# The state space part of a two-block kernel: 130 chunks of 8 tokens for 65 chunks of 16, a scan in two levels, and tables built between the first products

## The chip, the cores and the metric

One core of a Trainium2 chip runs the kernel. The metric is device time in microseconds of one execution; lower is better. The engines work side by side, each on its own queue in order, and meet at semaphores: TensorE (PE; its weight loads are PEld), VectorE (DVE), ScalarE (ACT), GpSimd (POOL) and SyncE (SP), which here only issues the weight loads.

## What is computed

Two transformer blocks on 1024 tokens of width 1024. The first puts 16 meta tokens ahead (so 1040 tokens), projects, runs causal differential attention on half of the width and a state space model on the other half, and mixes both. The part that the change touches is the state space model: 32 groups of 16 channels, 64 complex states each.

```python
def s5_ssm(u, a_re, a_im, log_dt, b_re, b_im, c_re, c_im, d_skip):
    dt = jnp.exp(log_dt)[:, None]
    mag, ang = jnp.exp(a_re * dt), a_im * dt
    ab_re, ab_im = mag * jnp.cos(ang), mag * jnp.sin(ang)
    ...                                   # bb = f * b, f from ab and a
    bu_re = jnp.einsum('blgh,gph->blgp', u, bb_re)
    bu_im = jnp.einsum('blgh,gph->blgp', u, bb_im)
    ...                                   # x_t = ab * x_(t-1) + bu_t, complex, by associative_scan
    y = (jnp.einsum('blgp,ghp->blgh', x_re, c_re) - jnp.einsum('blgp,ghp->blgh', x_im, c_im))
    y = y + d_skip.reshape(N_SSM_GROUPS, SSM_GROUP) * u
    return y.reshape(bsz, length, N_SSM_GROUPS * SSM_GROUP)
```

The queries and keys get a partial rotation (`rope`): out = t cos + rot(t) sin on the first quarter of each head. Behind both halves come a gated unit on y (glu), the mixing product, a feed-forward, and the second block (retention and RWKV-7, feed-forward, gate). None of these is changed.

## The kernel before

**Staging.** Activations lie in SBUF with features on partitions, split in a high and a low fp32r part (`act_hi`, `act_lo`); each large product is three passes over (high, high), (low, high), (high, low). Weights come as units of 128 x 1024 in the order `ORDER` through six slots (`SLOTS`); SP loads a unit when the one six places ahead of it is done, POOL splits it (`split_to`, L522 and L524). Every engine runs the same order of events, written out by hand: generators are advanced by the lists `PROJ_EVENTS` and `HEAD_EVENTS`, so an engine does its share of one event, then of the next. `give` starts an instruction and waits for its own end, `take` waits for another engine's.

**First stretch.** After the first norm, `PROJ` lists 29 products: u for 4 units with 3 spans each (512, 512 and 16 columns), v for 4 token tiles and the meta rows, then q and k for 8 units (one span for the first four, a second one of 16 columns for the others). Products rotate over three PSUM banks; ACT takes each out. A q or k unit is then rotated: PE multiplies `qk_raw` by `rot`, DVE makes `qk_o` out of it (`rotated`, three operations), ACT stores `qk_o` (L728). When the u units are stored, eight DMAs bring them back as `u_in` [128, 32 groups, 130], with 8 tokens x 16 channels on the partitions (L705).

**State space part, tables.** The groups are worked two to a pair of partition halves (16 pairs), four groups to a batch (`TB` = 8 batches). A chunk is `STEP` = 16 tokens, so there are 65 chunks, each of two octets. DVE discretises (`discretise`) and makes the powers `pw` of the state factor up to 16 (L2297 on). For each batch b:

- DVE `build_factors(b)`: `ca`, power times C for 17 lags, seven operations on 544 columns (L2084, L2087), after the store of the last one has landed;
- PE: impulse response kd = bb x ca, 16 instructions of 256 columns (L1478), then 8 transposes of the input factors `g_t` (L1489) that POOL makes (`input_factors`, L536);
- DVE copies kd out of PSUM, adds d_t (L2327 on), and copies the turned factors to `gt` (L2331); ACT stores `ca` and `kd` (L775, L778);
- PE: chunk inputs S = gt x u_in, 32 instructions of 65 columns (L1501); DVE copies them to `xs` (L2337).

In `PROJ_EVENTS` these stand after 15 products, as ssm, proj, ssm, proj for each batch.

**State space part, scan and output.** While attention's first half runs (`attention(0)`, 69 steps, with the far half of the v, q and k products between them, L1424 and L1676), DVE scans: for each chunk after the first, four operations on 32 columns (`wx`, `xs`), 63 times, in 8 parts, a part in every other attention step. Then, in every sixth step, PE makes a batch of output (L1520, L1522, L1524): for a group two blocks (even and odd octets), from `m_t` (shifted copies of kd, loaded by 8 DMAs a batch) and `ca2` (the stored `ca`) with `xs`; ACT copies `yb` out and stores it. An fp32 product is two instructions in the trace.

## Time and profile before

| | us |
|---|---|
| median of three runs | 3815.72 (3814.40 to 3825.63) |
| the profiled execution | 3815.3 |
| its span, first to last instruction | 3813.3 |
| PE busy | 3271.4 (86%) |
| PEld busy | 2539.4 (67%) |
| DVE busy | 1795.7 (47%) |
| ACT busy | 924.8 (24%) |
| POOL busy | 1995.2 (52%) |

Times in views of the trace count from the start of the span. A stretch's row gives busy time and in brackets the number of instructions for PE, PEld, DVE, ACT and POOL, then the granted clock (1.00 is 2.4 GHz, 0.50 is 1.2 GHz; between them a mix), the DMA share and GB/s. A row of a timeline gives start, length, engine, line, operation, output tile <- input tiles, shapes and count, and in brackets how long the engine had been idle and what ended it. Line 2084 is the helper for all of DVE's two-input operations, so the tile tells which it is; L626 is the same for ACT.

### The profile page before, as it was taken

What the parts mean: (1) busy time and instruction counts of PE and PEld (TensorE: products, weight loads), DVE (VectorE), ACT (ScalarE), POOL (GpSimd) and SP (SyncE); (2) the same over time, 40 slices, a digit from 0 to 9 for tenths busy, and PEclk for the clock granted to TensorE, in tenths of its full rate; (3) what the DMA queues carried; (4) which work ended last, traced back from release to release, by engine and by line L of the source; (5) the groups of instructions that cost most, each with busy time, mean ns of one, the idle gap of its engine ahead of it and who ended that gap; (6) DMA issues with size and microseconds to landing.
All of it is one profiled execution on the core that took longest, in us unless ns stands there. A gap on an engine that the chain in (4) does not pass through costs nothing.

```text
span 3813.3 us, 48913 instructions
## 1 busy us (share of the span) xinstructions
PE 3271.4 (86%) x19888; PEld 2539.4 (67%) x19888; DVE 1795.7 (47%) x2574; ACT 924.8 (24%) x1625; POOL 1995.2 (52%) x1076
## 2 busy tenths in 40 slices
PE   5874789569999785998889998898899998899997
PEld 4653466447777564776767776676677777678885
DVE  5366422233343354176556655257656556322233
ACT  3000111223233223213223332412223322210012
POOL 4452211225555463674655665565566665567773
PEclk9976677679999897999999999899999999999998
DMA  3521222222221232432222224232222222322221
GB/s 123 112 76 58 59 66 75 84 74 67 83 77 66 69 122 95 156 103 72 69 66 66 77 70 149 100 128 82 71 76 84 76 70 71 125 79 94 94 100 61
DMA packets 143856, 328.19 MB, mean 86 GB/s; under 512 B 25376, under 2 KB 62432, under 8 KB 143632
## 3 DMA queue, kind: packets, MB, share of 16 engines
q1 hardware_dynamic: 58752, 213.94, 16.8%
q10 hardware_dynamic: 84880, 111.12, 9.4%
q8 instruction: 158, 2.59, 0.3%
q14 instruction: 66, 0.54, 0.0%
HBM read 281.88 MB, written 43.12 MB: 85 GB/s over the span
## 4 chain that ended last, share of the span: by engine, by line
PE 72%; DVE 18%; ACT 4%; DMA 2%; ACTq 2%; issue 2%; POOL 0%; DVEq 0%; POOLq 0%
PE ps L1676 28%; PE ps L1705 11%; PE ps L1717 11%; PE ps L1907 3%; PE ps L1443 2%; PE ps L1540 2%; PE ps L1524 1%; DVE act_lo L2084 1%; DVE cab L2084 1%; DVE acc_dense L2084 1%; DVE wx L2084 1%; DVE ffh_lo L2713 1%; PE ps L1568 1%; PE ps L1520 1%; DVE rq L2084 1%
## 5 line engine op out<-in xcount | busy, mean ns | idle before, releaser
L522 POOL TENSOR_TENSOR w_hi<-w_raw,ones 128x1024 fp32r<-128x1024 f32 x408 | 807.7, 1980 | 1491.3 <-DMA w_raw<-weights 1477.3
L524 POOL TENSOR_TENSOR w_lo<-w_raw,w_hi 128x1024 fp32r<-128x1024 f32 x408 | 1005.1, 2464 | 32.0
L1676 PE MATMUL ps<-act_hi,w_hi 128*128 128x512 f32 x1696 | 709.3, 418 | 7.2 <-DVE act_lo L2084 6.6
L1676 PE MATMUL ps<-act_lo,w_hi 128*128 128x512 f32 x1696 | 683.7, 403 | 0.0
L1676 PE MATMUL ps<-act_hi,w_lo 128*128 128x512 f32 x1696 | 678.7, 400 | 0.0
L1676 PEld LDWEIGHTS ps<-act_hi,w_hi 128*128 128x128 f32 x1696 | 327.4, 193 | 101.0 <-issue 16.4
L1676 PEld LDWEIGHTS ps<-act_hi,w_lo 128*128 128x128 f32 x1696 | 327.0, 193 | 76.2
L1676 PEld LDWEIGHTS ps<-act_lo,w_hi 128*128 128x128 f32 x1696 | 326.8, 193 | 67.6 <-issue 1.7
L2084 DVE TENSOR_TENSOR acc_dense<-acc_dense,ps 128x512 f32<-128x512 f32 x352 | 242.1, 688 | 234.4 <-PE ps L1705 175.1
L1705 PE MATMUL ps<-w_hi,ffh_hi 128*128 128x512 f32 x704 | 295.4, 420 | 59.4 <-DVE acc_dense L2084 56.2
L626 ACT ACT_TABLE_LOAD x204 | 261.7, 1283 | 294.5 <-PE ps L1676 108.1
L1705 PE MATMUL ps<-w_hi,ffh_lo 128*128 128x512 f32 x704 | 281.8, 400 | 0.0
L1705 PE MATMUL ps<-w_lo,ffh_hi 128*128 128x512 f32 x704 | 281.3, 400 | 0.0
L1717 PE MATMUL ps<-w_hi,act_hi 128*128 128x512 f32 x640 | 264.0, 412 | 10.1 <-issue 5.6
L1717 PE MATMUL ps<-w_hi,act_lo 128*128 128x512 f32 x640 | 258.4, 404 | 0.0
L1717 PE MATMUL ps<-w_lo,act_hi 128*128 128x512 f32 x640 | 256.4, 401 | 0.0
L2709 DVE TENSOR_TENSOR ff_f<-ff_f,ps 128x512 f32<-128x512 f32 x88 | 60.5, 687 | 310.8 <-PE ps L1676 309.5
L1705 PEld LDWEIGHTS ps<-w_hi,ffh_hi 128*128 128x128 f32 x704 | 136.4, 194 | 101.3 <-DVE acc_dense L2084 67.3
L2173 DVE TENSOR_REDUCE small<-ps 128x1 f32<-128x144 f32 (+7 forms) x64 | 49.6, 775 | 303.3 <-PE ps L1542 303.2
L1705 PEld LDWEIGHTS ps<-w_lo,ffh_hi 128*128 128x128 f32 x704 | 136.3, 194 | 31.1
L1717 PEld LDWEIGHTS ps<-w_hi,act_hi 128*128 128x128 f32 x640 | 124.9, 195 | 43.8 <-issue 10.3
L1705 PEld LDWEIGHTS ps<-w_hi,ffh_lo 128*128 128x128 f32 x704 | 136.7, 194 | 25.7
(369 smaller groups left out, 4934.5 us busy)
## 6 DMA issues: line engine op xcount, KB each, us to landing
w_raw<-weights SPq DMA_DIRECT2D x408, 512.0 KB, 3.3
rw<-rw_t ACTq DMA_DIRECT2D x24, 256.0 KB, 2.2
rw<-lora_t ACTq DMA_DIRECT2D x24, 256.0 KB, 2.0
ca_scratch<-ca ACTq DMA_DIRECT2D x8, 544.0 KB, 2.9
ca<-ca_scratch ACTq DMA_DIRECT2D x8, 544.0 KB, 4.0
row<-x ACTq DMA_DIRECT2D x8, 512.0 KB, 3.3
m_t<-kd_scratch ACTq DMA_DIRECT2D x64, 64.0 KB, 3.5
row_dense<-x ACTq DMA_DIRECT2D x8, 512.0 KB, 3.9
```

Source lines behind the costliest of these rows:

```text
L522: pool.tensor_tensor(w_hi[:, s], raw, ones[:, 0:1].to_broadcast([P, 1024]), MUL).then_inc(w_hi_made, 1)
L524: pool.tensor_tensor(w_lo[:, s], raw, w_hi[:, s].bitcast(F32), SUB).then_inc(w_ready, 1)
L626: return act.activation(out, in_, func, **kw)
L1443: mm = pe.matmul(ps[:, n % 3, 0:c1 - c0], ws[w][:, u % SLOTS, P * k:P * k + P], acts[a][:, k, c0:c1], start=(k, w, a) == (0, 0, 0), stop=( ...
L1540: mm = pe.matmul(out[:, c:c + w], q, k[:, META + c:META + c + w], start=True, stop=True)
L1676: mm = pe.matmul(out, ws[w][:, s, P * k:P * k + P], acts[a][:, k, x], start=(k, w, a) == (0, 0, 0), stop=(k, w, a) == (KT - 1, 1, 0))
L1705: mm = pe.matmul(ps[:, 2 + n % 2, :], ffh[a][:, m % 4, P * k:P * k + P], ws[w][:, s, BANK * j:BANK * j + BANK], start=(m % 2, w, a) == (0, ...
L1717: mm = pe.matmul(ps[:, kinds[2] + k, :], source[a][:, 2 * uu + kk, x], ws[w][:, pos % SLOTS, BANK * kk:BANK * kk + BANK], start=(uu, kk, w ...
L1907: mm = pe.matmul(ps[head(c), 4 + b, n * u:n * u + n], lhs[head(c), u], rhs[head(c), u], start=True, stop=True)
L2084: give(dve.tensor_tensor(out, a, b, op), signal)
L2173: give(dve.tensor_reduce(small[:, col:col + 1], score_rows(h, u, br), X_AXIS, ALU.max, negate=True), s_max)
L2709: give(dve.tensor_tensor(ff_f[:, m % 2], ff_f[:, m % 2], ps[:, 1, :], MUL), ff_prod)
```

## The change

A chunk is now an octet of 8 tokens: 130 chunks, nine powers (`LAGS` 9), and one square impulse block of 128 x 128 to a group instead of a block of two octets. What follows from it, part by part:

- **Tables.** `ca`, `g_t` and `kd` are double. `ca` has 288 columns an operation, six operations with C negated beforehand (`c_n`). DVE builds batches 0 and 1 at once and batch b + 2 in event b. d_t is added on PE, by a small product with the identity; ACT copies kd, gt and xs out of PSUM. POOL splits 6 weight units (8 before) ahead of the first input factors, and up to unit 8 + b behind batch b (10 + b before).
- **Order.** The kd blocks go between the fourth and the twelfth product; three v products follow; then for each batch turn, state product, two projection products.
- **Scan.** 10 blocks of 13 chunks. First the powers of the chunk factor (`run_powers`), then 12 steps inside all blocks at once, nine steps over the block ends, then the ends spread into the blocks: 11 parts, one in each of the first 11 attention steps. ACT loads the first output tables only after the scan.
- **Output.** One block to a group: a product with `m_t` and two with `ca2`, 130 columns each, again one batch in every sixth step.
- **Rotation in place.** `qk_o` is gone; DVE rotates in `qk_raw`, and ACT, before it takes out a product of q or k, waits for the store of the unit two before.
- The loads of `u_in` go one v product earlier, with `rope`'s load behind them.

```diff
-STEP = 16
-NSTEP = L // STEP
 OCT = 8
 NOCT = L // OCT
+BLOCKS, RUN = 10, NOCT // 10
 PAIRS = GROUPS // 2
 GB = 8
-LAGS = STEP + 1
+LAGS = OCT + 1
...
-    PROJ_EVENTS = ["proj", "ssm"] + ["proj"] * 14 + ["ssm", "proj", "ssm", "proj"] * TB
+    PROJ_EVENTS = ["proj", "ssm"] + ["proj"] * 3 + ["ssm", "proj"] * TB + ["proj"] * 3 + ["ssm", "ssm", "proj", "proj"] * TB
     assert PROJ_EVENTS.count("proj") == len(PROJ) + 2
...
-        extra = ([["ssm"]] + [[]]) * (SCAN_PARTS + 1) + ([[]] * 5 + [["ssm"]]) * TB
+        extra = [["ssm"]] * (SCAN_PARTS + 1) + ([[]] * 5 + [["ssm"]]) * TB
...
-        split_to(8)
+        split_to(6)
         pool.wait_ge(factors_ready, 1)
         for b in range(TB):
             input_factors(b)
-            split_to(10 + b)
+            split_to(8 + b)
...
-                    if m == 2:
+                    if m == 1:
                         spills_landed(1)
                         for e in range(OCT):
                             act.dma_start(u_in[SG * e:SG * e + SG], t["u_scratch"][:, :, e, :].rearrange("m (g h) c -> h (m g) c", h=SG)).then_inc(ssm_landed, 16)
+                        act.dma_start(rope[:, :, :], t["rope"][:, :, 0:NEAR]).then_inc(const_landed, 16)
...
-                        act.wait_ge(rope_done, rope_index(m - 1, 0))
+                        store_turned(m - 2)
+                        act.wait_ge(qk_stored[m % 2], 16 * (m // 2))
                     act.wait_ge(*proj_done(n))
                     give(fn(qk_raw[:, m % 2, c0:c1], src, ACT.Copy, scale=QK ** -0.5 if m < 4 else 1.0), proj_kept)
...
+                if b:
+                    act.wait_ge(ca_stored, 16 * b)
+                    act.wait_ge(kd_stored, 16 * b)
+                act.dma_start(t["ca_scratch"][b], ca[:, b % 2]).then_inc(ca_stored, 16)
+                take(kd_psum)
+                for j in range(2):
+                    out = fn(kd[:, b % 2, j:TG:2, P:], ps[0:SG, 4 + 2 * (b % 2) + j, 0:2 * P].rearrange("p (g n) -> p g n", g=2), ACT.Copy)
+                    give(out, kd_ready if j else act_step)
+                act.dma_start(t["kd_scratch"][:, TG * b:TG * b + TG, :], kd[:, b % 2]).then_inc(kd_stored, 16)
+                yield
+            for b in range(TB):
+                q = slice(TQ * b, TQ * b + TQ)
+                take(g_turned)
+                give(fn(gt[:, :, :, :].rearrange("p q r n -> p (q r n)"), ps[:, 6, :], ACT.Copy), gt_ready)
...
+                take(ssm_s)
+                for ri in range(2):
+                    give(fn(xs[:, ri, q, 1:NOCT + 1], ps[:, 7 - ri, 0:TQ * NOCT].rearrange("p (q c) -> p q c", q=TQ), ACT.Copy), ssm_x if ri else act_step)
...
+            act.wait_ge(ssm_scanned, 1)
...
-                    rows, q = slice(SN * (g % 2), SN * (g % 2) + SN), g // 2
+                    rows, q, bank, c0 = slice(SN * (g % 2), SN * (g % 2) + SN), g // 2, 4 + 2 * (b % 2) + j % 2, P * (j // 2)
+                    skip = slice(SN * (g % 2), SN * (g % 2) + SG)
                     for ri in range(2):
-                        mm = pe.matmul(ps[0:SG, 4 + j % 2, 256 * (j // 2):256 * (j // 2) + 256], bb[rows, ri, q],
-                                       ca[rows, ri, q % TQ, 0:STEP, :].rearrange("p l h -> p (l h)"), start=ri == 0, stop=ri == 1)
+                        pe.matmul(ps[0:SG, bank, c0:c0 + P], bb[rows, ri, q], ca[rows, b % 2, ri, q % TQ, 0:OCT, :].rearrange("p l h -> p (l h)"),
+                                  start=ri == 0, stop=ri == 1)
+                    mm = pe.matmul(ps[0:SG, bank, c0:c0 + SG], ident[skip, skip], d_t[skip, q],
+                                   start=False, stop=True, skip_group_check=True)
                 post(mm, kd_psum)
+                yield
+            for b in range(TB):
                 pe.wait_ge(g_ready, b + 1)
+                pe.wait_ge(*((ssm_x, b) if b else (kd_ready, TB)))
                 for n in range(TQ):
-                    if b and n == 0:
-                        pe.wait_ge(gt_ready, TQ * (b - 1) + 1)
-                    if b and n == 1:
-                        pe.wait_ge(ssm_x, b)
-                    for half in range(2):
-                        for ri in range(2):
-                            mm = pe.transpose(ps[:, 6 + n, P * (2 * half + ri):P * (2 * half + ri) + P],
-                                              g_t[:, ri, n, OCT * half:OCT * half + OCT, :].rearrange("p s h -> p (s h)"), ident[:, :])
-                    post(mm, g_turned)
+                    for ri in range(2):
+                        mm = pe.transpose(ps[:, 6, P * (2 * n + ri):P * (2 * n + ri) + P], g_t[:, b % 2, ri, n].rearrange("p s h -> p (s h)"), ident[:, :])
+                post(mm, g_turned)
                 yield
                 if b == 0:
-                    pe.wait_ge(ssm_landed, 16 * (5 + OCT))
-                pe.wait_ge(gt_ready, TQ * (b + 1))
+                    pe.wait_ge(ssm_landed, 16 * (6 + OCT))
+                pe.wait_ge(gt_ready, b + 1)
                 for ri in range(2):
                     for n in range(TQ):
                         for par in range(2):
-                            rows, c0 = slice(SN * par, SN * par + SN), NSTEP * (TQ * ri + n)
-                            for half in range(2):
-                                mm = pe.matmul(ps[rows, 7, c0:c0 + NSTEP], gt[:, n, half, ri, rows],
-                                               u_in[:, TG * b + 2 * n + par, half:NOCT:2], start=half == 0, stop=half == 1)
+                            rows = slice(SN * par, SN * par + SN)
+                            mm = pe.matmul(ps[rows, 7 - ri, NOCT * n:NOCT * n + NOCT], gt[:, n, ri, rows], u_in[:, TG * b + 2 * n + par, :], start=True, stop=True)
                 post(mm, ssm_s)
...
+                    out = ps[:, 2 + j % 2, NOCT * (j // 2):NOCT * (j // 2) + NOCT]
+                    pe.matmul(out, m_t[:, j, :], u_in[:, g, :], start=True, stop=False)
+                    for ri in range(2):
+                        mm = pe.matmul(out, ca2[rows, ri, q % TQ, 1:LAGS, :].rearrange("p l h -> p (l h)"), xs[rows, ri, q, 0:NOCT], start=False, stop=ri == 1)
...
-            tt(qk_o[:, m % 2, c0:c1], qk_raw[:, m % 2, c0:c1], rope[:, 0, c0:c1], MUL)
-            tt(qk_o[:, m % 2, c0:c1], qk_o[:, m % 2, c0:c1], rope_sin_part[:, 0:c1 - c0], ADD, rope_done)
+            tt(qk_raw[:, m % 2, c0:c1], qk_raw[:, m % 2, c0:c1], rope[:, 0, c0:c1], MUL)
+            tt(qk_raw[:, m % 2, c0:c1], qk_raw[:, m % 2, c0:c1], rope_sin_part[:, 0:c1 - c0], ADD, rope_done)
...
+            if b >= 2:
+                dve.wait_ge(kd_psum, b - 1)
+                dve.wait_ge(ca_stored, 16 * (b - 1))
             lags = lambda ri: pw[:, ri, q, :].unsqueeze(3).to_broadcast([P, TQ, LAGS, SG])
-            chan = lambda ri: c_t[:, ri, q, :].unsqueeze(2).to_broadcast([P, TQ, LAGS, SG])
-            tmp = cab[:, :, :].rearrange("p a (q l h) -> p a q l h", q=TQ, l=LAGS)
-            cmul(ca[:, 0], ca[:, 1], lags(0), lags(1), chan(0), chan(1), tmp[:, 0], tmp[:, 1], negate_im=True, last=ca_ready)
+            chan = lambda c, ri: c[:, ri, q, :].unsqueeze(2).to_broadcast([P, TQ, LAGS, SG])
+            one, two = [cab[:, n].rearrange("p (q l h) -> p q l h", q=TQ, l=LAGS) for n in range(2)]
+            tt(one, lags(0), chan(c_t, 0), MUL)
+            tt(two, lags(1), chan(c_t, 1), MUL)
+            tt(ca[:, b % 2, 0], one, two, SUB)
+            tt(one, lags(0), chan(c_n, 1), MUL)
+            tt(two, lags(1), chan(c_n, 0), MUL)
+            tt(ca[:, b % 2, 1], one, two, ADD, ca_ready)
...
+        def run_powers():
+            give(dve.tensor_copy(px[:, 0, :, 0], a_step[:, 0, 0]), dve_step)
+            give(dve.tensor_copy(px[:, 1, :, 0], a_step[:, 1, 1]), dve_step)
+            wide = lambda v, n: v.unsqueeze(2).to_broadcast([P, PAIRS, n])
+            scratch = local[:, :].rearrange("p a r q i -> p a (r q i)")
+            for have, n in ((1, 1), (2, 2), (4, 4), (8, RUN - 8)):
+                tmp = scratch[:, :, 0:PAIRS * n].rearrange("p a (q h) -> p a q h", h=n)
+                cmul(px[:, 0, :, have:have + n], px[:, 1, :, have:have + n], wide(px[:, 0, :, have - 1], n), wide(px[:, 1, :, have - 1], n),
+                     px[:, 0, :, 0:n], px[:, 1, :, 0:n], tmp[:, 0], tmp[:, 1])
+            both_ways(a_run, px[:, :, :, RUN - 1], dve_step)
+
+        def scan_within(steps):
+            x = xs[:, :, :, 1:NOCT + 1].rearrange("p r q (i j) -> p r q i j", j=RUN)
+            now, other = local[:, 0], local[:, 1]
+            factor = lambda n: a_step[:, n].unsqueeze(3).to_broadcast([P, 2, PAIRS, BLOCKS])
+            for j in steps:
+                tt(now, x[:, :, :, :, j - 1], factor(0), MUL)
+                tt(other, x[:, ::-1, :, :, j - 1], factor(1), MUL)
+                tt(now, now, other, ADD)
+                tt(x[:, :, :, :, j], x[:, :, :, :, j], now, ADD)
+
+        def scan_ends(blocks):
+            now, other = wx[:, 0:2, :], wx[:, 2:4, :]
+            for i in blocks:
+                before, end = RUN * i, RUN * i + RUN
+                tt(now, xs[:, :, :, before], a_run[:, 0], MUL)
+                tt(other, xs[:, ::-1, :, before], a_run[:, 1], MUL)
+                tt(now, now, other, ADD)
+                tt(xs[:, :, :, end], xs[:, :, :, end], now, ADD)
+
+        def scan_spread(part, signal):
+            q = slice(4 * part, 4 * part + 4)
+            x = xs[:, :, q, 1:NOCT + 1].rearrange("p r q (i j) -> p r q i j", j=RUN)
+            shape = [P, 4, BLOCKS - 1, RUN - 1]
+            end = lambda ri: x[:, ri, :, 0:BLOCKS - 1, RUN - 1].unsqueeze(3).to_broadcast(shape)
+            power = lambda ri: px[:, ri, q, 0:RUN - 1].unsqueeze(2).to_broadcast(shape)
+            one, two = spread_tmp[:, 0], spread_tmp[:, 1]
+            for ri in range(2):
+                out = x[:, ri, :, 1:BLOCKS, 0:RUN - 1]
+                tt(one, end(ri), power(0), MUL)
+                tt(two, end(1 - ri), power(1), MUL)
+                tt(one, one, two, ADD if ri else SUB)
+                tt(out, out, one, ADD, signal if ri else dve_step)
...
+                if b + 2 < TB:
+                    build_factors(b + 2)
+                yield
+            for b in range(TB):
+                yield
+                yield
+            run_powers()
+            yield
+            dve.wait_ge(ssm_x, TB)
+            for part in range(4):
+                scan_within(range(1 + 3 * part, 4 + 3 * part))
+                yield
+            for blocks in (range(1, 6), range(6, BLOCKS)):
+                scan_ends(blocks)
```

## Rows read from the trace of the kernel before

**Rows 1.** By stretch: length; PE, PEld, DVE, ACT, POOL busy (instructions); clock; DMA share; GB/s.

```profile
57.00:132.00 75.00, 74.90 (x360) 62.37 (x360) 22.88 (x73) 12.68 (x17) 23.97 (x14) 0.98 0.27 75
132.00:311.00 179.00, 123.10 (x809) 85.58 (x808) 118.32 (x141) 7.29 (x15) 107.14 (x66) 0.80 0.36 89
...
324.00:414.00 90.00, 43.61 (x125) 29.55 (x126) 66.92 (x287) 9.15 (x33) 4.24 (x2) 0.59 0.06 22
414.00:442.60 28.60, 24.49 (x86) 15.31 (x86) 11.62 (x20) 5.90 (x20) 12.73 (x6) 0.80 0.38 103
442.60:688.20 245.60, 217.81 (x860) 162.50 (x858) 61.61 (x127) 35.58 (x113) 34.26 (x16) 0.70 0.22 64
```

**Rows 2.** TensorE's timeline: start us, length, line, operation, count, [idle before it <- releaser].

```profile
132.10 1.91 PE L1478 MATMUL ps<-ca,bb 64*16 64x256 f32 x16
...
151.46 2.06 PE L1501 MATMUL ps<-u_in,gt 128*64 128x65 f32 x32 [10.85 <-DMA u_in<-u_scratch]
...
300.11 3.60 PE L1478 MATMUL ps<-ca,bb 64*16 64x256 f32 x16 [17.05 <-DVE ca L2087]
...
323.97 0.79 PE L1540 MATMUL ps<-k_pair,q_pair 64*128 64x128 f32 x2 [6.78 <-DMA k_pair<-qk_scratch]
```

**Rows 3.** The chain of work from 0 to 700 us: start, length, what.

```profile
57.10 58.29 PE ps L1443 x288
...
182.95 5.59 PE ps L1443 x24
```

**Rows 4.** ScalarE's timeline, its DMA issues (ACTq) among it.

```profile
78.10 1.13 ACT L626 ACTIVATE u_t<-ps 128x512 f32<-128x512 f32 x1 [5.39 <-PE ps L1443]
...
129.36 9.24 ACTq L705 DMA_DIRECT2D u_in<-u_scratch  x8
...
152.06 0.60 ACT L626 ACTIVATE v_o<-ps 128x512 f32<-128x512 f32 x1 [12.81 <-DMA v_scratch<-v_o]
...
311.14 0.33 ACTq L728 DMA_DIRECT2D qk_scratch<-qk_o  x1
```

**Rows 5.** VectorE's timeline, around the end of the discretisation.

```profile
78.74 2.71 DVE L2084 TENSOR_TENSOR cab<-pw 128x64 f32<-128x64 f32 x2
...
81.75 0.62 DVE L2084 TENSOR_TENSOR cab<-pw 128x128 f32<-128x128 f32 x2
...
85.38 1.48 DVE L2084 TENSOR_TENSOR cab<-pw,c_t 128x544 f32<-128x544 f32 x2
```

**Rows 6.** GpSimd's groups, 56 to 312 us: count | busy us, mean ns | idle before.

```profile
L524 POOL TENSOR_TENSOR w_lo<-w_raw,w_hi 128x1024 fp32r<-128x1024 f32 x16 | 41.0, 2559 | 1.3
...
L536 POOL TENSOR_TENSOR g_tmp<-pw,bb 128x512 f32<-128x512 f32 x32 | 35.0, 1092 | 57.8 <-PE ps L1489 55.9
L522 POOL TENSOR_TENSOR w_hi<-w_raw,ones 128x1024 fp32r<-128x1024 f32 x16 | 34.5, 2159 | 75.6 <-DMA w_raw<-weights 75.1
```

**Rows 7.** The page's DMA issues: KB each, median us to landing.

```profile
ca_scratch<-ca ACTq DMA_DIRECT2D x8, 544.0 KB, 2.9
```

**Rows 8.** Groups from 324 to 443 us: a scan operation.

```profile
L2084 DVE TENSOR_TENSOR wx<-xs,a 128x32 f32<-128x32 f32 x126 | 26.7, 212 | 4.3
```

**Rows 9.** Busy time in stretches that are one output block each.

```profile
442.60:457.50 14.90, 14.90 (x59) 12.97 (x57) 0.00 (x0) 1.00 (x2) 4.25 (x2) 0.50 0.10 35
...
606.70:616.80 10.10, 10.10 (x59) 8.80 (x57) 4.33 (x5) 0.40 (x1) 3.77 (x2) 0.81 0.01 2
```

**Rows 10.** TensorE's timeline, fp32 products of 128 columns.

```profile
325.37 0.77 PE L1540 MATMUL ps<-k_pair,q_pair 64*128 64x128 f32 x2
...
331.91 0.47 PE L1540 MATMUL ps<-k_pair,q_pair 64*128 64x128 f32 x2
...
688.10 2.07 PE L1568 MATMUL ps<-v_pair,a_t 128*128 128x128 f32 x8
...
798.45 1.27 PE L1568 MATMUL ps<-v_pair,a_t 128*128 128x128 f32 x10
```

**Rows 11.** Waits from 414 to 693 us: in total, times, longest.

```profile
PE ps L1595 <- DVE o_n L2091: 24.6, 10, 10.1
```

157 lines of the change are left out of this document (59 added, 98 removed).

## The prediction

> **What bounds the kernel now.** I read the busy time by stretches first [rows 1]. The change touches the work up to about 688 us only; what stands behind it (glu, the feed-forwards, the second block: 3125 us) keeps its instructions, and I give it no change. Four stretches matter. From 57 to 132 TensorE is the bound (74.9 of 75.0 us busy with the u and v products). From 132 to 311 nobody is: PE is busy 123 of 179 us, DVE 118. There the state space tables are built group batch by group batch in a ring: DVE builds `ca`, PE multiplies, DVE copies out, ACT stores, DVE may build again. The last turn of this ring shows it: PE sat idle 17.05 us until DVE had written `ca` [rows 2]. From 324 to 414 DVE is the bound (66.9 us busy, and most of the rest it waits for the PE work of the attention steps): the 63 steps of the scan stand between the attention steps. From 442.6 to 688.2 PE is the bound (217.8 of 245.6 us), at a granted clock of 0.70, and the eight output blocks of the state space part (L1520, L1522, L1524) are the largest single thing in it.
>
> **Start, +1.** ACT's queue gets one more constant load (d_t in two halves of small pieces) ahead of the wait that lets the first norm begin. Bound: 0 to +3 us; I take +1, since a load costs about 0.5 us to issue there.
>
> **Projection, -21.** The tables' product blocks (kd) move from between the qk products to between the u products, the turns and state products stay, and copies go to ACT. I follow the new order on PE.
> The u products take 58.3 us for four units, so 14.6 for a unit, 5.6 for a product of 512 columns [rows 3]. Four products are done at 77.8 (ACT gets the fourth at 78.10) [rows 4]. Then the first kd block needs `ca`. Before, DVE began it at 85.38. The last power stage goes (L2084 128x128, from 81.75: 2.0 us); POOL no longer splits a weight unit meanwhile (it stops at 6 units and waits for the factors), which gives back 3.9 us (two operations on 64 columns took 2.71, two on 128 took 0.62) [rows 5]; `c_n` adds 0.3. So it begins at 79.8. Its six operations have 288 columns instead of 544 (0.74 each, half of 1.48): 0.46 each by the line through 128 and 544 columns. POOL starts the input factors at the same moment; I double them: 5.5 us. PE can go on at 85.3, having waited 7.5.
> A kd block: sixteen instructions of 128 columns for sixteen of 256, and eight small ones for d_t. The old block took 1.91 us at full clock and 3.60 at the low one [rows 2]. Bounds 1.4 to 4.0; I take 2.2, nearer the fast one, since PE comes from dense products: eight make 17.6. DVE builds two batches ahead into the double tables and has 5 to 8 us for each 3 to 5 us build, so PE shouldn't wait for it again. With 37.6 us of u products left, PE reaches the v products at 140.5 and has three of them at 157.
> Then it waits for the inputs `u_in`. Before, the loads were issued from 129.36 and had landed at 151.46, 22.1 us later [rows 2, 4]. Now they are issued behind the first v store, at about 149: landed at 171, and with ACT's copy of the turned factors the first state product starts at 172.5. This wait is as long as before (some 15 us); it hides nothing new.
> From there: state product 1.5 (the first of before took 2.06 with twice the instructions of half the columns), v3 5.6, the meta rows 6.5 (as many instructions, begun after a pause), to 186. Rounds 1 and 2 (turn 0.5, ACT copy 0.8, state product 1.5, two products 11.2, a rotation 0.9): 14.9 each, to 216. In rounds 3 to 5 a weight unit is late: POOL begins it only behind the input factors, and these behind the turn of the same round. Factors: six operations, the products 1.09 us at 512 columns, about 0.6 now, 3.8 in all; the split of a unit 2.16 + 2.56 [rows 6]: 8.5 us from the turn, of which PE covers 2.3. So 6 us of stall, 18.2 a round, to 271. Round 6 12.3, round 7 with two rotations 4, DVE 3: the last rotated piece is ready at 290, where before its store was issued at 311.14, 12.8 us ahead of the first scores at 323.97 [rows 2, 4]. So the scores start at 303 instead of 324: -21. Bounds: -35 (kd at 1.4, no unit late, `u_in` faster) to -3 (kd at 4, DVE doubled again by POOL, the stall 10).
> The moved copies: per batch 0.35 us twice for kd, 0.6 for gt, 0.35 twice for xs, on an engine that is busy 7.3 of 179 us [rows 1]; at nothing, except the 0.8 us in each round above, where PE waits for the copy. Behind ACT's new waits for stores to land stand its evacuations of products; the margin is a product's 5.6 us against a landing of 2.9 for the `ca` store [rows 7].
> By the Trainium skill, page "SBUF — State Buffer", section "SBUF: two separate sides", DVE with two SBUF inputs and GpSimd hold their common ports as an exclusive lock for a whole instruction. The trace agrees in kind [rows 5]. By that rule each of the six builds would wait out a POOL operation of about 2 us, the first `ca` would come 8 us later, and the sum below would be -47, so 3768.
>
> **Scan, +10.** Before: 63 steps of four operations on 32 columns, 0.212 each [rows 8]; with 0.035 between them 62 us of DVE. After: powers 30 small operations, 7.5; within blocks 12 steps of four operations on 320 columns at 0.50 + 0.035: 25.7; ends 9 steps of four on 32 columns: 8.8; spread 32 operations on 432 columns at 0.62 + 0.035: 21. Sum 63. Fewer instructions, as much time: the two-level form saves nothing on DVE. It also stands in 11 consecutive attention steps instead of every other of 16. Before, a part of 7.9 us covered the PE work of two steps; now one of 5.7 covers one, and the five steps after it have to be done in the open at some 4 us, as in the stretch from 414 to 442.6 (seven steps in 28.6 us) [rows 1]. 63 + 11 x 2 + 5 x 4 = 105 against 90 would be +15; some of the PE work is done at a better clock once it runs dense, so +10. Bounds 0 to +20. No other engine is behind it: POOL works 4.2 us there, so the operations run undisturbed.
>
> **Output blocks, -52.** The eight blocks stand between 442.6 and 688.2; from first to last instruction they take 98.7 us together, between 10.1 and 15.0 each (two of them in [rows 9]). A block has 56 matrix instructions of 65 columns (an fp32 product is two), 0.18 to 0.27 us apiece; now it has 24 of 130 columns. What costs is mostly the instruction with its 128 weight columns, not the columns streamed: L1568, with 128 streamed columns, took 1.27 us for ten at full clock and 2.07 for eight at the low one, so 0.13 and 0.26, no more than the blocks' 0.18 and 0.27 with 65. The upper bound is L1540, in pairs, not in long runs: 0.24 and 0.38 [rows 10]. At the clock mix of before a block costs 4.8 to 7.6 us; I take 5.8, nearer the long runs: 46 instead of 98.7, -52, bounds -60 and -38.
> **Handed back, +7.** While PE did a block the other engines caught up: DVE was idle in all of the first and in 5.8 of 10.1 us of the sixth [rows 9]. With blocks half as long a few waits come out again; PE's waits for DVE's normed output (L1595) are 24.6 us from 414 to 693 now [rows 11]. I take a quarter of that; bounds 0 to +15. The blocks also come six steps earlier, which changes nothing at the end, since the last attention step ends the stretch.
> The copies of the results, their stores and the table loads keep their number; rotating in place saves no operation.
>
> **Sum.** +1 - 21 + 10 - 52 + 7 = -55, against the profiled execution's 3815.3 us: 3760. That execution lies 0.4 us below the median shown, so the forecast is the same against it. The bounds, taken as independent, give 3736 to 3784.
>
> **The rivals.**
> Waits come back in full: the attention steps have a chain of their own (scores, maximum, exponent, difference, turn), and with less PE work between they become the bound. For it: L1595 and L1540 wait already. Against it: PE is busy 217.8 of the 245.6 us [rows 1]. Output gain -25 instead of -45 net: 3780 to 3790. Chance 0.12.
> Columns rule: a block is paid by what it streams, 7 x 65 columns a group before and 3 x 130 after, 14% less. That gives -14 instead of -52: 3798. L1568 speaks against it [rows 10]. This is how the Trainium skill has it ("TensorE: Matmul & The Clock Gate", "Step-by-step: what each phase is for": time by columns fed in, the weight load behind it). Chance 0.08.
> Better clock: the first block ran at a granted clock of 0.50, 1.2 GHz, the one at 606.7 at 0.81 [rows 9]. If the new blocks, and the products behind them, keep 2.4 GHz, a block costs 4.4 instead of 5.8 and some 45 us of products at the low clock lose 20: -30, so 3730. Chance 0.06.
> Slower: rotating in place makes ACT wait, before it takes out a qk product, until the store of two products ago has landed. ACT works in order, and behind this wait stand the copies for the state part and, later, the exponents of attention. One landing behind the `u_in` loads took ACT 12.8 us (v_o at 152.06) [rows 4]. If stores land like that, each of the 12 units pays about 7: +84, 3844. It decides from a landing of about 6 us on. Chance 0.05.
> The forecast itself: 0.69.
>
> **Range and chances.** 3725 to 3797 takes in the bounds, the clock case and the returning waits. A change of under 0.3% (11 us) can't be told from none. Faster than 3804: 0.88; within: 0.07 (half of the columns case with the scan at its upper bound); slower than 3827: 0.05.
>
> **What would show it.** First scores near 303; PE idle before the first kd block about 7 and before the first state product about 14; weight units late in three rounds; 63 us of DVE scan in 11 steps; output blocks of 4 to 8 us. Wrong would be: first scores later than 320, blocks over 10, or attention steps that take as long as before without the blocks' work.

## The result, and the profile of the changed kernel

The changed kernel takes 3779.6 us (median, 3773.2 to 3783.4), beside 3815.1 for the kernel before on the same chip: ratio 0.990, interval 0.988 to 0.992. It is 35 us faster, where the forecast had 55. The profiled executions say the same: spans of 3776.3 and 3813.3. The time lies in the range, but it is the sum of one large miss and of smaller ones that mostly make up for it, and the large one is the part worth learning from.

The changed kernel by stretches, as in [rows 1]. The second runs to the wait for the inputs of the state products, the third is that wait, the fourth runs from there to the first scores, the fifth to the first output block, the sixth to the last attention product. Columns: length; busy time of PE, PEld, DVE, ACT and POOL (instructions); granted clock; DMA share; GB/s.

```profile
57.70:161.10 103.40, 97.94 (x481) 72.46 (x482) 46.27 (x108) 17.06 (x31) 22.03 (x18) 0.81 0.20 59
161.10:182.00 20.90, 19.53 (x76) 15.52 (x76) 0.00 (x0) 0.80 (x2) 1.21 (x2) 0.88 0.73 117
182.00:196.50 14.50, 0.00 (x0) 0.00 (x0) 0.00 (x0) 1.79 (x3) 6.94 (x7) 0.54 1.01 131
196.50:346.00 149.50, 108.98 (x534) 83.50 (x534) 26.04 (x36) 18.36 (x38) 72.95 (x54) 0.79 0.24 80
346.00:446.00 100.00, 48.47 (x150) 32.90 (x151) 77.01 (x185) 10.79 (x38) 4.40 (x3) 0.60 0.10 32
446.00:650.60 204.60, 169.24 (x672) 114.66 (x670) 69.61 (x143) 39.92 (x129) 45.88 (x22) 0.82 0.22 66
```

The kernel before, its last two of these stretches, first scores to first block and first block to last attention product:

```profile
324.00:442.60 118.60, 68.10 (x209) 44.86 (x210) 78.55 (x307) 15.06 (x53) 16.97 (x8) 0.64 0.14 41
442.60:690.20 247.60, 219.81 (x868) 164.28 (x866) 61.61 (x127) 35.98 (x114) 34.26 (x16) 0.70 0.23 64
```

First scores came at 346.0 instead of 324.0 [rows 2]: 22 us later, where the forecast had 21 earlier. From there to the last attention product it took 304.6 us instead of 366.2: 61.6 less, where the forecast had 35. Behind that 2.6 us more (3125.7 against 3123.1), which I did not follow. It is within what one execution differs from the next: the same stretch takes 3120.0 us in e6 and 3126.0 in e10. So 22.0 - 61.6 + 2.6 = -37.0, the difference of the spans.

What PE waited for in the changed kernel, from the start of the projections to the first scores (time in all, times, longest):

```profile
PE ps L1512 <- ACT gt_s L626: 21.7, 8, 15.9
PE ps L1455 <- POOL w_lo L524: 21.3, 4, 7.7
PE ps L1478 <- DVE qk_raw L2088: 7.9, 2, 5.3
PE ps L1491 <- DVE ca_s L2088: 5.4, 1, 5.4
```

Two kd blocks on PE in the changed kernel: the first product pair and its small d_t pair of the block at 88.61, of the block at 100.98, and what followed the first block. The old block of sixteen took 1.91 at full clock and 3.60 at the low one [rows 2].

```profile
88.61 1.03 PE L1491 MATMUL ps<-ca_s,bb_s 64*16 64x128 f32 x4 [5.42 <-DVE ca_s L2088]
89.56 0.23 PE L1493 MATMUL ps<-d_t_s,ident 16*16 16x16 f32 x2
...
93.08 0.80 PE L1455 MATMUL ps<-act_hi,w_hi 128*128 128x512 f32 x1
93.68 0.63 PE L1455 MATMUL ps<-act_lo,w_hi 128*128 128x512 f32 x1
...
100.66 0.39 PE L1455 MATMUL ps<-act_hi,w_lo 128*128 128x512 f32 x1
100.98 0.61 PE L1491 MATMUL ps<-ca_s,bb_s 64*16 64x128 f32 x4
101.52 0.21 PE L1493 MATMUL ps<-d_t_s,ident 16*16 16x16 f32 x2
```

A group of six starts every 0.68 us at full clock and every 1.12 at the low one, so a block is 2.78 or 4.55, and the eight took 27.2 (26.6 counted from start to start, since the tail of each lies under the next product). The first product behind the first block began at 0.63 an instruction instead of 0.39 and took 8.0 us instead of 5.8.

The low clock also comes without any kd block. The fourth u product stands behind a narrow one, ahead of the first block; it ran at the low clock in the changed kernel (8.6 us) and at full clock in e1 (5.8), which has the same order there:

```profile
75.16 0.63 PE L1455 MATMUL ps<-act_lo,w_hi 128*128 128x512 f32 x1
```

```profile
73.85 0.40 PE L1455 MATMUL ps<-act_lo,w_hi 128*128 128x512 f32 x1
```

Two output blocks at full clock and one at the low one in the changed kernel, against the first block of before (442.6, 14.9 us, also [rows 9]):

```profile
445.90:450.10 4.20, 4.20 (x27) 3.22 (x25) 3.82 (x4) 0.39 (x1) 4.12 (x3) 1.00 0.36 125
469.20:473.40 4.20, 4.20 (x27) 3.16 (x25) 0.00 (x0) 0.98 (x2) 0.54 (x1) 1.00 0.40 125
572.80:580.40 7.60, 7.60 (x27) 5.56 (x25) 0.00 (x0) 0.39 (x1) 2.79 (x2) 0.50 0.07 25
```

Seven of the eight output blocks took 4.21 and one 7.48: 36.9 together, where before they took 98.7.

### The profile page after: what moved, and what is told of

Same layout as the page of the kernel before. It is cut to its first block, busy times and chain, and to the rows that moved or that the text cites. A ratio compares the mean times of both kernels' runs of the same rounds, so it can differ in the third digit from the quotient of the medians.

```text
span 3776.3 us, 48065 instructions
## 1 busy us (share of the span) xinstructions
PE 3229.1 (86%) x19536; PEld 2501.1 (66%) x19536; DVE 1729.2 (46%) x2399; ACT 940.8 (25%) x1665; POOL 1967.0 (52%) x1076
## 4 chain that ended last, share of the span: by engine, by line
PE 73%; DVE 16%; ACT 4%; ACTq 2%; issue 2%; DMA 2%; POOL 1%; DVEq 0%; POOLq 0%
PE ps L1680 29%; PE ps L1709 12%; PE ps L1721 11%; PE ps L1911 3%; PE ps L1455 3%; PE ps L1544 2%; DVE acc_dense L2088 1%; DVE act_lo L2088 1%; DVE ffh_lo L2761 1%; PE ps L1572 1%; ACTq L883 1%; DVE xn_dense L2095 1%; DVE local L2088 1%; DVE rq L2088 1%; PE ps L1618 1%
## 5 line engine op out<-in xcount | busy, mean ns | idle before, releaser
L522 POOL TENSOR_TENSOR w_hi<-w_raw,ones 128x1024 fp32r<-128x1024 f32 x408 | 799.3, 1959 | 1406.4 <-DMA w_raw<-weights 1392.2
L1721 PEld LDWEIGHTS ps<-w_hi,act_hi 128*128 128x128 f32 x640 | 124.6, 195 | 44.3 <-issue 10.3
```

The source lines that it names most:

```text
L522: pool.tensor_tensor(w_hi[:, s], raw, ones[:, 0:1].to_broadcast([P, 1024]), MUL).then_inc(w_hi_made, 1)
L1721: mm = pe.matmul(ps[:, kinds[2] + k, :], source[a][:, 2 * uu + kk, x], ws[w][:, pos % SLOTS, BANK * kk:BANK * kk + BANK], start=(uu, kk, w ...
```

## The experiments

Line numbers are those of the changed kernel. "First scores", "first block" and "end" are the first score product, the first output block and the last product of values in the first attention half: 346.0, 445.9 and 650.6 in the changed kernel. Times are medians and places are those of the profiled execution, which can lie 10 us beside its median (3759.6 in e1, 3735.7 in e2, 3697.1 in e7).

**e1: weight units split further ahead.** Does the late weight unit cost what its row says?

```diff
         for b in range(TB):
             input_factors(b)
-            split_to(8 + b)
+            split_to(10 + b if b else 8)
```

> The changed kernel, with POOL splitting two more weight units ahead of each input factor batch from the second on, as the kernel before did. In the changed kernel PE waited four times, 21.3 us together, for the low half of a weight unit between the first state product (196.6) and the first scores (346.0), and the product behind each wait ran 7 to 8.4 us at the low clock instead of 5.6. Theory (late units cost what the row says): the waits for w_lo go, the products behind run at 5.6, first scores near 320, time near 3755. Rival (another wait stands right behind them: the turned factors, or the rotation's copy of qk): the idle time changes its releaser, first scores 335 to 346, time 3765 to 3780.

Measured: 3750.0 us (ratio to before 0.983, 0.981 to 0.984), 30 less than the changed kernel. The row for `w_lo` is gone from PE's waits, first scores come at 321.3 (24.7 earlier), the end at 632.1 (18.5 earlier). The waits stood for 21.3 of the 24.7. The theory holds, and no other wait took their place. Between first scores and first block 5.5 us came back: PE is busy 53.6 us there for 48.5, with the same 150 instructions at a clock of 0.56 for 0.60. Why the clock is lower was not traced.

**e2: kd blocks behind the u products.** Where do they cost least, and what do the inputs of the state products wait for?

```diff
-    PROJ_EVENTS = ["proj", "ssm"] + ["proj"] * 3 + ["ssm", "proj"] * TB + ["proj"] * 3 + ["ssm", "ssm", "proj", "proj"] * TB
+    PROJ_EVENTS = ["proj", "ssm"] + ["proj"] * 11 + ["ssm", "proj"] * TB + ["ssm", "ssm", "proj"] * TB + ["proj"] * 3
...
-            split_to(8 + b)
+            split_to(12 + max(b - 1, 0) if b else 8)
```

> As the run before it (POOL further ahead, by two more units), and the eight kd blocks stand behind u product 12: between the v products and the first three qk products, no longer between the u products; the turn and state products follow with one projection product each. Theory (a kd block of 128-column instructions lets the clock fall, and the next dense product pays 1.5 to 2.7 us for it; and the inputs of the state products are fetched only when the last u product is stored, so whatever stands in front of that delays them): the twelve u products take 68 us, end near 126 instead of 161, the 14.5 us of idle time ahead of the first state product go, the kd blocks still cost 2.7 to 4.5 each in their new place, first scores near 300, time near 3735. Rival (the same PE work in any order; only the idle 14.5 us go): first scores 10 to 15 us before those of the first run. Rival (slower): DVE's table builds and POOL's factors now meet the turns, so the state products come late and the gain over the first run is 0.

Measured: 3730.1 us (ratio 0.977, 0.975 to 0.980). PE in this run, from the u products' start to their end, to the first turn, to the first scores:

```profile
57.70:115.10 57.40, 57.36 (x288) 48.42 (x288) 27.62 (x72) 11.25 (x14) 21.82 (x18) 1.00 0.19 56
115.10:198.30 83.20, 76.13 (x389) 49.98 (x389) 22.60 (x39) 10.90 (x25) 12.76 (x6) 0.88 0.63 134
198.30:292.00 93.70, 74.20 (x416) 58.16 (x414) 27.39 (x33) 16.02 (x35) 70.08 (x56) 0.83 0.27 89
```

and its wait for the turned factors (time in all, times, longest):

```profile
PE ps L1512 <- ACT gt_s L626: 6.1, 8, 0.8
```

The twelve u products take 57.4 us at a clock of 1.00, where in the changed kernel they took 71.2 of the 103.2 us (from start to start), at 0.81. The eight of them that stand behind the first kd block there took 45.7, and 35.9 here. (My 68 in the expectation counted the four narrow ones, 16 columns and 2.8 us each, as full.) The kd blocks, now between the v and the first qk products, take 2.78 in six of eight cases and leave the products behind them at 5.83; the low clock shows behind the stall for `ca` (4.55, then 7.8) and behind the first block. The idle 15.9 us ahead of the first state product are gone: `u_in` lands under the v products. Relative to e1 the first scores come 29.3 us earlier and the time is 20 us less. In the profiled execution the part behind the first half took 3139.3 us, 13 to 19 more than in the other runs named here; that was not traced. (e2 also lets POOL split further ahead than e1 does; neither has PE wait for a weight unit.)

**e3: output products in halves.** Is an output block paid by its instructions or its columns?

```diff
-                    out = ps[:, 2 + j % 2, NOCT * (j // 2):NOCT * (j // 2) + NOCT]
-                    pe.matmul(out, m_t[:, j, :], u_in[:, g, :], start=True, stop=False)
+                    for c0 in (0, NOCT // 2):
+                        c1 = c0 + NOCT // 2
+                        out = ps[:, 2 + j % 2, NOCT * (j // 2) + c0:NOCT * (j // 2) + c1]
+                        pe.matmul(out, m_t[:, j, :], u_in[:, g, c0:c1], start=True, stop=False)
```

and the two `ca2` products in the same loop.

> The changed kernel, with each product of an output block in two halves of 65 columns: twice the instructions, the same columns. The blocks took 4.2 us at the mixed clock for 24 instructions, 37 us for all eight. If an instruction costs the same with 65 columns as with 130 (the forecast's reading), a block takes 8 to 9 us, all eight 66 to 75, and the last attention product ends 20 to 35 us later. If a block is paid by its columns, it stays at 4.2 to 5, and nothing moves.

Measured: one execution of 3822.4 us; the blocks take 88.1 us together, more than the 66 to 75 expected, and the end is 42 us later. Three of them:

```profile
449.90:460.80 10.90, 10.90 (x51) 9.34 (x49) 5.49 (x5) 0.39 (x1) 7.37 (x4) 0.64 0.15 50
519.40:532.60 13.20, 13.20 (x50) 11.30 (x48) 1.26 (x2) 0.99 (x2) 4.24 (x2) 0.50 0.13 41
672.60:681.60 9.00, 9.00 (x50) 7.82 (x49) 0.00 (x0) 0.39 (x1) 2.33 (x1) 0.81 0.01 2
```

At the same granted clock of 0.50: 48 instructions of 65 columns 13.2 us (0.275 each), 24 of 130 columns 7.48 (0.312 each), and 56 of 65 columns in the kernel before 14.9 (0.266 each). Half the columns save 12% of an instruction. PEld, the weight load, is busy 11.3 of the 13.2 us, and 5.6 of 7.6 with 130 columns. So the instruction count is the main price, and PEld's share says that the loading of its 128 weight columns is nearly all of a 65-column instruction. The rest of the factor of 2.4 is the clock: none of these blocks ran at 1.00, seven of eight did in the changed kernel.

**e4 and e5: the scan left out, after and before.** What does it cost on the path in each form?

```diff
# e4, on the changed kernel
-            for part in range(4):
-                scan_within(range(1 + 3 * part, 4 + 3 * part))
-                yield
...
+            for part in range(10):
+                if part == 9:
+                    give(dve.tensor_copy(xs[:, 0, :, 2], xs[:, 0, :, 1]), ssm_scanned)
+                yield
# e5, on the kernel before
-                for c in range(1 + SCAN_RUN * part, min(1 + SCAN_RUN * (part + 1), NSTEP - 1)):
+                for c in ([NSTEP - 2] if part == SCAN_PARTS - 1 else []):
```

> The changed kernel with the scan left out (the steps within blocks, the block ends and the spreading; the powers stay; the state enters the outputs unscanned). It prices the scan on the path. By the forecast an attention step costs 4 us in the open, so the 86 us from the first scores to the first output block become 48: 38 us less, for 63 us of DVE work taken away. Rival: DVE is the bound through and through, 60 us less. Rival: the gap is given back by the steps behind, under 20 us less.

> The kernel before with the scan left out but for its last step (the state enters the outputs unscanned). It prices the old scan on the path, beside the changed kernel without its scan, where the first output block came 56 us earlier for 63 us of DVE work. In the kernel before, the first block came 118.6 us after the first scores (323.97, 442.61). By the forecast the old scan, on every other attention step, was covered better: 18 steps at 4 us are 72, so 46 us less. Rival: it stood on the path like the new one: 56 or more less. Rival: the PE work between hid most of it: under 30 less.

Measured: 3718.9 and 3762.0 us (one execution each). The stretches from first scores to first block and on to the end, first of e4, then of e5:

```profile
345.60:389.90 44.30, 39.05 (x149) 27.59 (x150) 19.03 (x70) 10.79 (x38) 4.40 (x3) 0.81 0.22 68
389.90:594.70 204.80, 169.46 (x673) 114.78 (x671) 69.44 (x143) 39.92 (x129) 45.87 (x22) 0.82 0.22 66
```

```profile
322.30:386.70 64.40, 57.36 (x209) 38.71 (x210) 23.15 (x59) 15.08 (x53) 16.99 (x8) 0.79 0.25 74
386.70:640.40 253.70, 225.57 (x868) 169.29 (x866) 61.60 (x127) 36.04 (x114) 34.25 (x16) 0.67 0.22 62
```

The first block comes 55.6 us sooner behind the first scores without the new scan (99.9 to 44.3; 7 us of powers stay in), and 54.2 sooner without the old one (118.6 to 64.4). DVE work taken away: 58.0 and 55.4. My 38 and 46 were too low in both: up to the first block the scan stands on the path with nearly its whole DVE time. In the changed kernel nothing is given back behind the block: 204.6 us with the scan and 204.8 without. In the kernel before it is 253.7 without against 247.6, and 5.8 of these 6.1 us are PE's busy time, for the same 868 instructions at a clock of 0.67 for 0.70.

**e6: the scan parts on every other attention step.**

```diff
-        extra = [["ssm"]] * (SCAN_PARTS + 1) + ([[]] * 5 + [["ssm"]]) * TB
+        extra = ([["ssm"]] + [[]]) * (SCAN_PARTS + 1) + ([[]] * 4 + [["ssm"]]) * TB
```

> The changed kernel, with the eleven scan parts and the first table load on every other attention step, as in the kernel before, and the output blocks every fifth step instead of every sixth so that all fits. If the eleven steps in a row cost the 10 to 15 us that the forecast gives them, the last attention product of the first half comes 10 to 15 us earlier than 650.6. If DVE is the bound either way and its 55 us stand on the path wherever the parts are, it moves by less than 5.

Measured: 3779.7 us (one execution), the end at 657.9, 7 us later than in the changed kernel, with the first scores 1 us earlier. Neither reading held: it came neither 10 to 15 us earlier nor within 5. The 10 to 15 us that the forecast gives to the eleven steps in a row don't show. That the end is later may come from the closer output blocks; the run does not separate it.

**e7 and e8: the scan taken off the path.** If the scan is pure DVE time on the path, the place for it is where DVE is idle: 26.0 busy of 149.5 us ahead of the first scores.

```diff
# both: powers ahead of the turns, five scan events moved from the attention to the projections; e7 on e2, e8 with e1's split; e8's order:
+    PROJ_EVENTS = ["proj", "ssm"] + ["proj"] * 5 + ["ssm", "proj"] * 3 + ["proj"] * 3 + ["ssm", "proj"] * 5 + ["ssm", "ssm", "proj"] * TB + ["ssm"] + ["proj", "ssm"] * 4 + ["proj"] * 2
-        extra = [["ssm"]] * (SCAN_PARTS + 1) + ([[]] * 5 + [["ssm"]]) * TB
+        extra = [["ssm"]] * (SCAN_PARTS + 1 - 5) + ([[]] * 5 + [["ssm"]]) * TB
```

> The second run's kernel (kd blocks behind the u products, POOL further ahead; 3730), and the scan begins as soon as the last states are there: the powers are built ahead of the turns, and four scan parts stand on DVE around the last projection products instead of behind the first attention steps. DVE was idle in most of that stretch (about 258 to 292). If the scan on the path is all DVE time, the 28 us of these parts that now run there come off: the first output block follows the first scores by about 70 instead of 98 us, and the time is near 3705. Rival: the last rotations stand behind a scan part on DVE, so the first scores come 7 to 10 us later and half of the gain goes: 3715 to 3720.

> As the run before it, but in an order that gives the scan parts PE work to run under: three kd blocks between the u products, five between the v products, then the eight turns and state products with one qk product each, then four scan parts each with a qk product. PE has the same work; the last state product comes about 25 us earlier in it. If the kd blocks between u products cost only the fall of the clock (about 2 us each) and DVE keeps up, first scores near 295, the first output block about 60 us behind them, time near 3695. Rival: u_in comes 9 us later and the turns wait for it again, so it is no better than the run before: 3705 or more.

Measured: e7 3708.3 us (ratio 0.971, 0.968 to 0.974), e8 3697.2 (0.968, 0.966 to 0.971). The medians are 11 us apart, but the single times overlap (3697 to 3712 and 3691 to 3706). In both the first block comes at 377, 12 to 13 us ahead of e2's and 69 ahead of the changed kernel's. In e7 the first scores slipped to 311.3 (e2: 292.0), as the rival had it, by 19 us for its 7 to 10. In e8 they slipped to 324.0, not the 295 of my expectation: PE waits 28.3 us in four stretches for rotations that stand behind scan parts on DVE. The scan gained more than the scores lost. The end falls from 594.6 (e2) to 574.1 and 568.8.

**e9: kd blocks without the small d_t products.** Which instructions make the block dear?

```diff
-                    mm = pe.matmul(ps[0:SG, bank, c0:c0 + SG], ident[skip, skip], d_t[skip, q],
-                                   start=False, stop=True, skip_group_check=True)
```

> The changed kernel without the eight small d_t instructions of each kd block (the skip term D is left out of the output). A kd block took 2.78 us at full clock and 4.55 at the low one, for sixteen instructions of 128 columns and eight of 16; the block of the kernel before took 1.91 and 3.60 for sixteen of 256. If each instruction has the same price whatever it streams, the block falls to 1.85 at full clock and 3.0 to 3.6 at the low one, and the v products begin 8 to 15 us earlier than 160.9. If the small ones are nearly free and the 128-column ones are dear, it stays at 2.5 or more.

Measured: one execution of 3763.7 us; the v products begin at 142.7 instead of 160.9. Two blocks of it, at the low and at the full clock:

```profile
88.56 1.90 PE L1491 MATMUL ps<-ca_s,bb_s 64*16 64x128 f32 x16 [8.64 <-DVE ca_s L2086]
...
97.84 1.06 PE L1491 MATMUL ps<-ca_s,bb_s 64*16 64x128 f32 x16
```

Neither reading held. Sixteen 128-column instructions take 1.06 and 1.90, about half of the sixteen 256-column ones of before (1.91, 3.60): these, with 16 weight columns, are paid by the columns they stream. The eight 16-column instructions between them cost the other 1.7 at full clock and 2.7 at the low one, 0.21 and 0.33 each, three times a 128-column instruction of the same block. Each writes into the bank that the group before it has just written, with another weight shape; which of the two makes it dear is open. The v products begin 18.2 us earlier: 16.2 are the blocks' own (10.4 for 26.6, from start to start), the rest is the clock of the products between.

**e10, e11 and e12: all of the scan ahead of the attention.**

```diff
# e10: e8's powers and split; no kd block beside a narrow u product; all scan events among the projections
+    PROJ_EVENTS = ["proj", "ssm"] + ["proj"] * 6 + ["ssm"] + (["proj"] * 3 + ["ssm"]) * 2 + ["proj", "ssm"] * 5 + ["ssm", "ssm", "proj"] * TB + ["ssm"] + ["proj", "ssm"] * 2 + ["proj"] * 3 + ["ssm"] * 8
# e11: e10, and the first eight pairs scanned within blocks during the last four turns
+                if b >= 4:
+                    dve.wait_ge(ssm_x, 4)
+                    scan_within(range(1 + 3 * (b - 4), 4 + 3 * (b - 4)), 0)
# e12: e10 with ["ssm"] * 4 at the end, the spreading back between attention steps
```

> The run e8's order (3697), with two changes: no kd block stands beside a u product of 16 columns any more, and all ten scan parts stand on DVE ahead of the attention, two of them between the last projection products and eight behind. In e8 DVE sat idle 13.7 us ahead of the first scores while six scan parts were still to come between the attention steps. Expected: the scan ends near 325, attention then runs without it, the first output block comes near 350 instead of 377, time near 3680. Rival: PE then stands idle and at a low clock until the scan is done, and as the attention steps begin later the gain is only the 14 us of idle time: 3683 to 3690. Rival (slower): the first attention steps are held back more than the scan parts cost between them: 3697 or more.

> As e10, with the scan within blocks done in two halves of eight pairs: the first half from the fifth turn on, under the state products and qk products, where DVE was idle 47 of 69 us; the second behind the last state product. 48 more DVE operations of half the size. Expected: 320 elements took 0.73, 160 should take near 0.45, so 20 us go under the products and the rest of the scan is 20 us shorter: time 12 to 15 us below e10. Rival: the rotations wait behind the early parts, PE waits for the rotations, and the state products slip: no better than e10.

> As e10 (3685), with the last four scan parts (the spreading) back between the first attention steps; the steps within blocks and the block ends stay ahead of the attention. In e10 PE stood idle 26.4 us between the first scores and the end of the scan. Expected: the spreading parts, 5.5 us each, cover the chain of the first four steps (3.7 each, of which DVE works 1.6), so some 8 us less: 3677. Rival: the steps are held back by as much as they are covered, 3685 as before. Rival (slower): the first output block comes later and the end with it: 3690.

Measured: e10 3685.5 us (ratio 0.966, 0.963 to 0.970), first block at 348.0, end at 560.1. That is 94 us less than the changed kernel and 3.4% less than the kernel before. The rival for e10 came closest: PE stands idle 26.4 us until the scan is done, so 12 of the expected 17 us were had. e12 gives 3686.7 (0.967, 0.964 to 0.969), no different from e10.

e11 gives 3696.8 (0.970, 0.967 to 0.974): 11 us slower, on DVE work that was put where DVE was idle. DVE and POOL at the same time, in e11:

```profile
239.78 2.01 DVE L2088 TENSOR_TENSOR xs<-xs,local 128x160 f32<-128x160 f32 x1
241.82 4.24 DVE L2088 TENSOR_TENSOR local<-xs,a_step 128x160 f32<-128x160 f32 x2
246.09 2.35 DVE L2088 TENSOR_TENSOR local<-local 128x160 f32<-128x160 f32 x1
...
257.25 0.32 DVE L2088 TENSOR_TENSOR local<-local 128x160 f32<-128x160 f32 x1
257.61 0.43 DVE L2088 TENSOR_TENSOR xs<-xs,local 128x160 f32<-128x160 f32 x1
```

```profile
241.57 2.34 POOL L524 TENSOR_TENSOR w_lo<-w_raw,w_hi 128x1024 fp32r<-128x1024 f32 x1
243.87 1.97 POOL L522 TENSOR_TENSOR w_hi<-w_raw,ones 128x1024 fp32r<-128x1024 f32 x1
245.92 2.34 POOL L524 TENSOR_TENSOR w_lo<-w_raw,w_hi 128x1024 fp32r<-128x1024 f32 x1
```

While POOL splits weight units, each DVE operation takes as long as the POOL operation beside it (2.35 and 2.34), five to seven times its own 0.32 to 0.43. POOL is hardly slowed by DVE operations this short: `w_hi` takes 1.97 for the 1.90 that it takes elsewhere in e11, `w_lo` 2.34 for 2.34. Beside DVE's longer operations it is: in the kernel before, while DVE builds `ca` (0.72 us an operation when alone), `w_hi` takes 2.37 and `w_lo` 2.70, against 1.89 and 2.36 a few us later:

```profile
287.37 2.74 DVE L2084 TENSOR_TENSOR ca<-cab 128x544 f32<-128x544 f32 x1
```

```profile
286.84 2.70 POOL L524 TENSOR_TENSOR w_lo<-w_raw,w_hi 128x1024 fp32r<-128x1024 f32 x1
289.50 2.37 POOL L522 TENSOR_TENSOR w_hi<-w_raw,ones 128x1024 fp32r<-128x1024 f32 x1
```

In e11 the rotations queue up behind and PE waits 16.3 us for one. The Trainium skill says this on the page "SBUF — State Buffer", section "SBUF: two separate sides": DVE and GpSimd take their common ports as an exclusive lock for a whole instruction. Here the trace agrees in size too.

## Why the prediction was right, and where it was wrong

The sign and the largest gain were right: the output blocks, paid by instruction, and twice as fast. The sum missed by 18 us, and that it missed by so little is luck in part: the projection came out 43 us above its term and far outside its bounds (-35 to -3), and the clock, the scan and the output blocks together 27 below theirs. The prediction's own sign of being wrong, "first scores later than 320", came true at 346. Its bounds, taken as independent, also give 3740 to 3786 and not 3736 to 3784. Term by term:

**Start.** +1 forecast, +0.6 measured (57.74 against 57.10 in [rows 3]).

**Projection: -21 forecast, +21.5 measured. This is the term that failed.** Its miss of 43 us falls into three steps.
- "I take 2.2 [...] eight make 17.6", and "With 37.6 us of u products left, PE reaches the v products at 140.5": it reached them at 160.9, 20.4 later. The first block began 3.3 late. The blocks took 9.0 more (26.6, from start to start), for the eight small instructions that I had as good as left out (e9). And the u products behind the first block took 45.7 us for 37.6. I priced the inserted block and not what comes of its neighbours. In the changed kernel it stood beside u products of 16 columns, and from such a pair of short pieces on the clock was low into the next product (8.4 us instead of 5.8 behind the third block). Between full products (e2, e8, e10) it mostly stayed at 1.00. A narrow product can do it without a block: the fourth u product took 8.6. That one cost nothing, since PE then waited for `ca`; in e1, e4 and e6 it took 5.8, and the v products began at 160.7 to 160.8 all the same.
- The wait for `u_in`, "(some 15 us); it hides nothing new", was 15.9 and cost 4 us more than forecast with the v products before it. What the step did not say is that the wait could be avoided: in e2 it is 0.8. The loads hang on the last u product, and the change puts 27 us of kd work ahead of that.
- "So 6 us of stall, 18.2 a round, to 271. Round 6 12.3": four rounds had a late unit, not three, and they took 16.7, 22.0, 21.5 and 24.2. The stalls were 1.2, 7.75, 6.2 and 6.2. The product behind the short one took 5.8, but those behind the other three took 7.6 to 8.4, and three later state products 2.0 instead of 1.1. I counted the idle time and not the clock behind it. 149.5 us from first state product to first scores, for 130.5.

**Scan, +10, and handed back, +7: +8.6 measured, between them.** From first scores to the end, PE was idle 366.2 - 287.9 = 78.3 us before and 304.6 - 217.7 = 86.9 after. e4 and e5 split it only in part: without either scan the idle time still grows by 5.4 (35.2 to 40.6). But e4 keeps the powers, 7 us of DVE work behind the first scores that e5 does not have, so the 5.4 is at most what the shorter blocks hand back, and no run separates the two. The rest of the scan adds little (55.6 against 54.2). Of the four operations of a step on 320 elements, the three that touch `xs` took 0.70 to 0.71 and only the fourth my 0.50 (0.49); the ends and the spreading came out a little below forecast, and the DVE time came out as forecast (58 and the powers). What was wrong is the cover: the forecast let the old scan hide the PE work of two steps and the new one that of one. Up to the first block both scans are nearly wholly open (e4, e5), and spreading the new one gained nothing (e6).

**Output blocks, -52 forecast, -61.8 measured.** The reading was right (e3: twice the instructions, 1.76 times the time at the same clock). The block took 4.21, below my bound of 4.8 (I took 5.8), because the blocks ran at a clock of 1.00 where those of before had 0.50 to 0.81. At an equal clock the gain is two to one.

**Better clock: chance 0.06, and behind the first scores it is in part what happened.** Besides the blocks PE was busy 189.2 us in this stretch before and 180.8 after, for the same instructions: -8.4. With the blocks' 10 us below forecast that is 18 of the 30 us of this rival. Ahead of the first scores the clock went the other way.

Sum: 0.6 + 21.5 - 61.8 + 8.6 - 8.4 + 2.6 = -36.9.

**The other rivals.** Columns rule: refuted for the output blocks by e3, and true for the kd products (e9). That the weight load decides between the two is read from PEld's busy time; no run changes the weight columns alone. The rule of the Trainium skill that the prediction named ("TensorE: Matmul & The Clock Gate", "Step-by-step: what each phase is for") thus agrees with the kd products (0.119 us for 256 columns, 0.066 for 128) and not with the output blocks (0.312 for 130, 0.275 for 65). The same section has the weight load's time grow with the columns of the weights, and that agrees: 128 of them in the output blocks, 16 in the kd products. Waits in full: no, 5.4 us at most. ACT waiting for the stores of rotated rows: in the changed kernel no wait of ACT for `qk_scratch` shows from 196 to 650 us; before each product's copy it waits for PE (81.7 us in 12 waits). Undoing the rotation in place alone was not tried. Such a wait appeared once in e7 (16.0 us) and once in e8 (13.9). DVE's six operations for the first `ca` took 5.9 us beside POOL, near my doubled 5.5 and not 8 us more. That does not speak against the rule of the Trainium skill ("SBUF — State Buffer", "SBUF: two separate sides") that the prediction named: POOL's operations there are mostly short ones (0.7 to 0.95 us), and the one DVE operation that met a weight split took 2.03 beside its 1.99. The kd block began at 88.6 for my 85.3 because the table copies and two memsets that I had left out (0.91 the longer) stand ahead of the build.

## What to carry to other kernels

Price a moved block with its neighbours: in this kernel stalls of 5 us and more, and runs of short matrix instructions, were often paid a second time by the dense product behind them, which began at half the clock. Before calling a wait unavoidable, ask which issue it hangs on and what the change puts in front of that; and put the work of an engine that is the bound later into its idle time earlier, but not beside a stream of long POOL operations (e11). Here the change's own gain was 35 us, and reordering the same instructions gave 94 more.

## What the runs showed of the hardware that I had not expected

- An fp32 instruction with 128 weight columns costs 0.275 us with 65 streamed columns and 0.312 with 130 (both at the low clock); one with 16 weight columns costs 0.119 with 256 streamed columns and 0.066 with 128 (full clock).
- A 16-column product between 128-column groups costs 0.21 us at full clock, more than three of its neighbours.
- Two-input DVE operations of 0.32 us take 2.35 beside POOL's 2.34, one for one, while POOL keeps its pace (e11). DVE operations of 0.72 us slow POOL as well: 1.89 to 2.37 and 2.36 to 2.70 (the kernel before).
